# RWKV loops: the gate's side work at every fourth turn instead of every second

## The reference

```python
proj = h @ w_in[l]
gate_cols, mla_cols, rwkv_cols, conv_cols = _split(proj, [GATE_COLS, MLA_COLS, RWKV_COLS, CONV_COLS])
o_a = mla_branch(...) @ mla_w_o[l]
o_b = rwkv7_branch(...) @ rwkv_w_o[l]
o_c = short_conv_branch(conv_cols, conv_w[l]) @ conv_w_o[l]
g = jax.nn.sigmoid(gate_cols).reshape(bsz, seq, N_BRANCH, D_MODEL)
merged = g[:, :, 0] * o_a + g[:, :, 1] * o_b + g[:, :, 2] * o_c
```

```python
sa = jnp.einsum('bhvk,bhk->bhv', state, a_t)
state = state * w_t[:, :, None, :] + sa[..., None] * b_t[:, :, None, :] + v_t[..., None] * k_t[:, :, None, :]
y_t = jnp.einsum('bhvk,bhk->bhv', state, r_t)
```

## Time and profile before

| | us |
|---|---|
| median of three runs | 4294.44 (4288.24 to 4296.98) |
| the profiled execution, own time | 4293.35 |
| its span | 4291.6 |
| loops of layer 0, first power step of chunk 0 to the product behind chunk 3 | 2572.07 to 2747.98 |
| loops of layer 1, the same | 3629.86 to 3802.92 |

### The profile page before, as it was taken

The page is one execution under the profiler, slowest core; times in us unless marked ns, Lnnn a source line. Parts: engine busy times, 40 slices in busy tenths (PEclk is TensorE's granted clock), DMA queues, the critical chain, the costliest instruction groups (busy, mean ns, idle before and its releaser), DMA issues.

```text
span 4291.6 us, 52426 instructions
## 1 busy us (share of the span) xinstructions
PE 3877.6 (90%) x21392; PEld 3031.0 (71%) x21392; DVE 1863.1 (43%) x2812; ACT 1324.7 (31%) x1963; POOL 431.7 (10%) x277
## 2 busy tenths in 40 slices
PE   7788878999998999899978889899998888889999
PEld 3555546788886777688865667678886565767887
DVE  2544443533334434544444354543433435454433
ACT  3332322322223322333333431232232333123222
POOL 0211110000001111000021121000001122000000
PEclk9878888999998999899989999999999999999999
DMA  4112243121211221232211221033221121113232
GB/s 161 55 46 79 89 173 103 50 69 60 69 48 52 79 94 65 78 106 93 87 45 42 56 70 40 25 101 97 92 94 38 45 72 46 38 37 108 91 97 69
DMA packets 320319, 317.02 MB, mean 74 GB/s; under 512 B 8720, under 2 KB 286128, under 8 KB 319952
## 3 DMA queue, kind: packets, MB, share of 16 engines
q1 hardware_dynamic: 320080, 313.67, 23.1%
HBM read 311.55 MB, written 2.10 MB: 73 GB/s over the span
## 4 chain that ended last, share of the span: by engine, by line
PE 79%; DVE 12%; ACT 5%; issue 1%; DMA 1%; POOL 1%; DVEq 0%; SPq 0%; ACTq 0%; POOLq 0%
PE PS L132 78%; DVE scr L146 5%; ACT scr L142 3%; DVE scr L156 1%; DVE scr L164 1%; DMA ring<-in_ada_w 1%; ACT L142 1%; PE PS L135 1%; DVE NBt L156 1%; DVE scr L168 1%; DVE PS L160 0%; DVE scr L176 0%; DVE NBt L146 0%; DVE scr L172 0%; DVE ffn_h L156 0%
## 5 line engine op out<-in xcount | busy, mean ns | idle before, releaser
L132 PE MATMUL PS<-scr 128*32 128x32 f32 (+7 forms) x6692 | 662.7, 283 | 156.6 <-DVE scr L146 89.7
L132 PEld LDWEIGHTS PS<-scr 128*128 128x128 f32 (+4 forms) x6692 | 542.0, 170 | 305.2 <-issue 118.1
L132 PE MATMUL PS<-ffn_h,ffn_w 128*128 128x512 f32 (+1 forms) x3168 | 616.3, 357 | 7.8 <-DVE ffn_h L156 5.7
L132 PEld LDWEIGHTS PS<-ffn_h,ffn_w 128*128 128x128 f32 x3168 | 524.6, 189 | 100.5 <-issue 9.0
L142 ACT ACTIVATE scr<-PS 128x256 f32<-128x256 f32 (+5 forms) x425 | 193.5, 455 | 823.0 <-PE PS L132 752.9
L132 PE MATMUL PS<-h_h,ring_r 128*128 128x512 f32 (+1 forms) x976 | 357.6, 429 | 35.8 <-POOL ring_r L146 22.0
L142 ACT ACTIVATE scr<-scr 128x256 f32<-128x256 f32 (+7 forms) x404 | 212.5, 526 | 519.5 <-DVE scr L156 322.4
L132 PE MATMUL PS<-mlp_h,mlp_w 128*128 128x512 f32 x1536 | 361.3, 396 | 0.0
L132 PE MATMUL PS<-mlp_g,mlp_w 128*128 128x512 f32 x1536 | 359.7, 396 | 0.0
L132 PEld LDWEIGHTS PS<-mlp_h,mlp_w 128*128 128x128 f32 x1536 | 288.4, 188 | 70.5 <-issue 1.0
L132 PEld LDWEIGHTS PS<-mlp_g,mlp_w 128*128 128x128 f32 x1536 | 288.5, 188 | 69.9
(11 more groups left out here) (151 smaller groups left out, 4757.6 us busy)
## 6 DMA issues: line engine op xcount, KB each, us to landing
ring<-in_ada_w SPq DMA_DIRECT2D x48, 1024.0 KB, 6.1
ring<-in_ffn_w_in SPq DMA_DIRECT2D x44, 1024.0 KB, 5.1
ring<-in_w_up SPq DMA_DIRECT2D x32, 1024.0 KB, 5.4
ring<-in_w_down SPq DMA_DIRECT2D x32, 1024.0 KB, 5.0
ring<-in_w_in SPq DMA_DIRECT2D x60, 512.0 KB, 3.9
ring<-in_ffn_w_out SPq DMA_DIRECT2D x16, 1024.0 KB, 5.1
scr<-in_na_bias SPq DMA_DIRECT2D x32, 512.0 KB, 5.0
ring<-in_na_w_qkv SPq DMA_DIRECT2D x24, 512.0 KB, 4.3
```

The source lines that it names most:

```text
L132: return self.eng.matmul(o, lhsT=l, rhs=r, start=start, stop=stop) if self.eng else Nothing()
```

## The change

The rate of the side work in the two loops goes from 0.5 to 0.25, on every engine at once.

```diff
     def rw_turns(chain, loop, beside):
         weave((chain, 1), beside=(beside, 3))
-        weave((loop(0), 1), (loop(1), 1), beside=(beside, 0.5))
+        weave((loop(0), 1), (loop(1), 1), beside=(beside, 0.25))
         weave(beside=(beside, 1))
         run(beside)
```

## The result

| | before | after |
|---|---|---|
| median | 4294.44 us (4287.54 to 4297.92, 5 runs) | 4312.24 us (4311.15 to 4323.08, 5 runs) |
| ratio, 95% interval | | 1.005 [1.0035, 1.0065] |
| span of the profiled execution | 4291.6 | 4310.4 |

The change made the kernel slower by 17.8 us. The sign is as forecast. The size is 8 us over the 4304 predicted and just outside the range that ended at 4312.

The account below looks back on a forecast made before the run. TensorE, busy 90% of the span, was taken as the bound, with VectorE bounding the mask stages. Terms 7.5+2.8+0 = +10.3 us on the profiled 4293.35 gave 4303.7, stated as 4304; range 4295 to 4312.

Parts of the forecast that it names:

- Term 2: Clock of TensorE after waits ahead of the power steps: lower clock costs 13.0 us instead of 10.2, +2.8 (-2.6 to +5.0).
- Term 1: Mask stages of both layers: their length less the side work in them grows by +7.5 us (+3.6 to +10).
- the collision with GpSimd in chunk 2: GpSimd's 2.4 to 2.8 us product moves into chunk 2's mask stage and slows a VectorE product there: +1.0 us taken.
- Term 3: TensorE's waits between steps outside the mask stages: as many covered as uncovered, taken as 0 (-2.6 to +2.6 us).
- VectorE's stall at turn 32: Chunk 1's mask stage: an output product between first and second heads' products makes VectorE wait 2.45 us, stage 12.5 us.
- the price of a fall: Start of power steps at 1.2 GHz: 1.9 us after long waits, 1.1 in chunk 0, from the first 40 records.
- the line drawn from short to long waits: Clock cost by wait ahead of the power steps: 0.64 us for 2.0 to 2.5 us waits, 1.9 for long ones.
- the missing 2.3 us: Stretches between power steps of successive chunks: 14.9 us of side work but 12.6 difference; most of the gap called clock.
- (a): Rival for the whole kernel: no change, the spread work hides as well as before; +1 us, 4294; chance 0.20.
- (b): Rival: faster by the clock alone, with a quarter in each mask stage keeping it up; 4284 to 4288; chance 0.08.
- (c): Rival: much slower, all terms at upper ends, VectorE stalled and GpSimd collision a full lock; +17.6, 4311; chance 0.06.
- (d): Rival: the change doesn't do what it says; excluded because side work now stands in chunk 2; no chance given.

Follow-up runs that it names:

- turn 33: Rate 0.25 as in the changed kernel, but chunk 1's output product comes one loop turn later, behind the second heads' products: 4301.55 us, 1.0017 of the kernel before.

## Why the prediction was wrong in size

**Which steps failed.** Two terms of the sum were too small. Term 2, the clock, was put at +2.8 us and measured +6.9 in the profiled execution, +5.0 over three: a fall was priced too low, and a wait of 4.4 us was priced well below a long one. Term 1 has "I take +1.0" for the collision with GpSimd in chunk 2, which measured 1.95 in each layer. The rest of the miss is 0.5 us in Term 3, 3.4 outside the loops and 0.7 from the rounding of the forecast: 4304 is 9.6 above the median before, the terms add up to 10.3.

**The picture was right.** The mask stages belong to VectorE, side work outside them is paid in full, and the change takes side work out of them. The experiments that fill the stages show it in the strongest way (-43 us), and the outcome lies on the side that the forecast named.

**Term 1, mask stages: +7.5 predicted, +9.0 measured** (65.7 to 74.7; as idle time +8.6). Stage by stage for layer 0: chunk 0 9.7 predicted, 9.2 measured (its quarter ran partly at 1.2 GHz and took 2.1); chunk 1 8.9 and 8.9, with the length of 12.5 predicted and 12.56 measured; chunk 3 8.45 and 8.5. VectorE's stall at turn 32, reckoned as 2.45, stands in its timeline as 2.61:

```profile
2615.74 0.69 DVE L146 TENSOR_TENSOR scr<-PS,NBt 128x512 f32<-128x512 f32 x1 [2.61 <-PE PS L132]
```

The collision in chunk 2 is the part that failed. VectorE's and GpSimd's rows there, after:

```profile
2661.57 0.69 DVE L146 TENSOR_TENSOR scr<-PS,NBt 128x512 f32<-128x512 f32 x1 [0.42 <-PE PS L132]
2662.29 2.63 DVE L146 TENSOR_TENSOR scr<-scr 128x512 f32<-128x512 f32 x1
2665.03 0.69 DVE L146 TENSOR_TENSOR scr<-PS,NBt 128x512 f32<-128x512 f32 x1
```

```profile
2662.01 2.37 POOL L146 TENSOR_TENSOR ring_r<-ring,ring_r 128x1024 fp32r<-128x1024 f32 x1 [4.46 <-ACT ring_r L142]
```

VectorE's product with both inputs in SBUF was issued 0.28 us behind GpSimd's and ended only after it: 2.63 us instead of 0.69. The experiment that moved GpSimd's product away took 1.95 off the stage in each layer (of which the loops, by the clock, kept 1.7 over both). The +1.0 had been drawn from the mildest row, 1.47, where the VectorE product was issued 1.85 us behind a GpSimd product of 2.77. The kernel before had a dearer one in its very first stage, beside GpSimd's 2.35 us from 2561.70 on:

```profile
2562.72 1.88 DVE L146 TENSOR_TENSOR scr<-scr 128x512 f32<-128x512 f32 x1
```

In all these rows (1.47, 1.84, 1.88, 1.93 and 2.63) the VectorE product ended 0.5 to 0.6 us after GpSimd's. So what such a meeting costs is set by what is left of GpSimd's product when VectorE's is issued. The Trainium skill (SBUF — State Buffer, "Who interferes with whom") calls it an exclusive lock held for the whole instruction, and the row agrees; the prediction had weighed this and priced it at 2.8 us more, of which 1.9 came.

**Term 2, the clock: +2.8 predicted, +6.9 measured in that execution, +5.0 over three.** Two of its steps were off. The first is the price of a fall: 7.43 less 5.37 over the first 40 records, with the 5.37 taken from chunk 0 for chunks 2 and 3. Chunks 2 and 3 at 2.4 GHz need 4.7 to 4.8 us for them, as the kernel with the extra matmuls shows, and the whole fall there cost 2.4, not 1.9. The second is the line drawn from short to long waits, which gave 1.35 to a wait of 4.4 us. The waits of 4.55 and 4.57 us in layer 1 and layer 0 cost nearly what 6.13 cost. Windows of 12 us behind them, layer 0 chunk 1 and layer 1 chunks 0 and 1:

```profile
2621.58:2633.58 12.00, 11.84 (x72) 0.77 0.00 1
...
3638.81:3650.81 12.00, 12.00 (x61) 0.77 0.01 3
3686.15:3698.15 12.00, 11.83 (x71) 0.75 0.00 0
```

A share of 0.77 means 5.5 of these 12 us at 1.2 GHz, and at most half of that lost, 2.8 us (at 0.76 the extra matmuls won back 2.4). Before, the windows at the same three places had 0.86, 1.00 and 1.00. But the length of the wait does not order the costs either. Chunk 3's start in layer 0, behind 4.87 us of idle, has this window:

```profile
2722.94:2734.94 12.00, 11.79 (x68) 0.87 0.28 89
```

That is at most 1.6 us, near the 1.45 that the line gave. The same wait of 4.86 or 4.87 us had 0.86 to 0.88 in all six such starts of the kernel after's three executions, and 0.75 to 0.77 in the four of the two kernels with the halving moved. By the windows the starts of the kernel after cost at most:

| chunk | priced per layer | at most, layer 0 and 1 |
|---|---|---|
| 0 | 1.9 | 2.5, 2.8 |
| 1 | 1.35 | 2.8, 3.0 |
| 2 | 1.8 | 2.8, 3.1 |
| 3 | 1.45 | 1.6, 1.7 |

The largest miss is chunk 1. By the same measure the starts of the kernel before cost at most 14.4 us, those of the kernel after 20.2; the 6.9 of busy time holds 1.1 more than this difference. That the upper bound of +5.0 equals the measured mean is luck: it came from eight falls at 1.9, against starts that differ by a factor of two. What makes two starts behind the same idle time differ stays open. The Trainium skill (TensorE: Matmul & The Clock Gate, "What's actually happening") states that the monitor's window is free-running. The repeated executions of the kernel before agree: 2.50 us of idle with opposite results.

**Term 3, waits between steps: 0 predicted, +0.5 measured.** The wait of 0.64 us in chunk 1 is gone, and one of 0.58 us came up in chunk 0.

**The signs it named.** The waits of chunks 1 to 3 came near what was foretold (4.57, 6.49 and 4.87 in layer 0, for 4.4, 5.8 and 4.8), chunk 1's stage and stall as well. Chunk 0's did not. It was to be about 6 us, and under 4 would have been a sign of being wrong. It is 4.01 and 4.55, and 3.89 in a repeated execution of layer 0, because a part of the idle time lies ahead of the last `LL` product:

```profile
2567.76 0.48 PE L132 MATMUL PS<-scr 64*128 64x128 f32 x2 [1.55 <-DVE scr L146]
...
2574.37 7.07 PE L132 MATMUL PS<-scr 128*128 128x128 f32 x40 [4.01 <-DVE scr L146]
```

The text had read the wait as stage less work, in one piece. What chunk 0 cost in layer 0 lies between 1.5 us (its first 40 records took 6.91 against 5.37) and the 2.5 of the table, so its price of 1.9 was not far off. A smaller reading was off too: between the earlier trace rows's two stretches the clock accounts for about half of the missing 2.3 us (0.93 of 53.31 and 0.88 of 40.67), not for most.

**Outside the sum.** With 1.5 us more in Term 1, 2.2 more in Term 2 and 0.5 in Term 3 the predicted 10.3 becomes 14.5, and the loops lost 14.4 over three executions. The medians differ by 3.4 more. In the profiled pair 2.8 us lie outside the loops; over all executions the stretch outside them runs from 3913.2 to 3934.7 us, without relation to the edit (the fastest kernel has the longest). I put the 3.4 down to this spread; that was not tested by itself.

**The rivals.** (a) and (b) are out: neither the idle time nor the clock was kept. (c), much slower at 4311, comes nearest, and both mechanisms that it named were there: the stall at turn 32 and the full lock. But its sum was not met term by term. Term 1 stayed under its upper end, Term 3 far under, Term 2 went past it in the profiled execution, and 3.4 of the 17.8 us lie outside the loops, so that its number fits is in part luck. Its chance of 0.06 was too little: the stall stood in the forecast already, and the earlier trace rows and the 1.88 above spoke for the lock. (d) was excluded rightly. The layer forecast (layer 1 loses more) came true: +9.3 against +6.7.

## What to carry to other kernels

Side work belongs into the stretches where another engine is the bound, in the amount that fits. A rate can't do that, a list of turns can; here it was worth 43 us together with the moved halving, while halving the rate cost 18. When side work moves, look up beside it what else rides on the same turn: a VectorE product of two SBUF inputs issued during a GpSimd product ended 0.5 to 0.6 us after it, so it costs up to nearly the length of GpSimd's (1.94 of 2.37 us here). Price a fall of TensorE's clock as up to half the time spent at 1.2 GHz, read from windows behind the wait, not over a fixed number of records whose duration at 2.4 GHz is taken from elsewhere, and not by the length of the wait alone.

## What the runs showed of the hardware

- Work whose result nobody reads can pay: 96 further instructions in idle stretches of TensorE kept the clock at 2.4 GHz behind them and made the kernel 6 us faster.
- Idle time of one length had opposite effects on the clock in two executions of the same program (2.50 us: 1.00 and 0.86 over the next 12 us). Of the six starts behind 2.46 to 2.50 us in the three executions of before, four fell; the three behind 1.98 and 1.99 us all fell, one behind 2.17 fell, two behind 2.21 and 2.35 did not. In the other kernels two more behind 1.98 and 1.99 us went either way (0.86 and 1.00, the kernel with extra matmuls), the four behind 2.80 and 2.81 us all fell (turn 33, alone and with the halving moved), and behind 1.12 us neither of two fell.
- A longer wait is not always a dearer one: behind 4.57 us the next 12 us had 0.77, behind 4.87 in the same execution 0.87.
- The clock can also fall without a long wait: in the kernel with extra matmuls it did so once in each chunk 3, amid the joining of blocks (76 records in 11.74 and 11.73 us instead of 10.10).
- A VectorE product of two SBUF inputs issued while GpSimd's ran took 1.47 to 2.63 us instead of 0.69 and ended 0.5 to 0.6 us after GpSimd's.
- The start of the loops lay anywhere from 2557.74 to 2577.16 us over fourteen executions, in front of which no kernel differs from another. A difference of a few us between two profiled spans says nothing until it is placed in a stretch that the edit touches.
